# Gate rows by way of DRAM, the convolution's copies, taps and mean, and the low weight parts at the end of the recurrence, in a transformer block with convolution and HGRN2 layers

## The reference

```python
def forgetting_attention(q, k, v, f_logit):        # 8 heads of 64
    logf = jax.nn.log_sigmoid(f_logit)
    c = jnp.cumsum(logf, axis=1)                    # one running sum per head
    logits = q @ k.T * scale + c[query] - c[key]    # causal
    ...

def first_block(...):
    proj = rmsnorm(x) @ w_in                        # 3592 columns: q, k, v, 8 gates, q, k, v
    y = concat(forgetting_attention(...), chunked_relpos_attention(...))   # 8 + 8 heads
    x = x + rmsnorm(y @ w_out)
    x = x + rmsnorm(memory_cross_attention(...))    # 4 heads of 256, 256 memory rows
    x = x + rmsnorm(square(relu(rmsnorm(x) @ w_ff1)) @ w_ff2)              # 4096 wide

def conformer_conv(h, w_in, dw_w, dw_b, ln_g, ln_b, w_out):
    a, gate = jnp.split(h @ w_in, 2, axis=-1)
    u = a * jax.nn.sigmoid(gate)
    y = depthwise_conv(u, dw_w, width=31) + dw_b    # each channel by itself
    y = jax.nn.silu(layer_norm(y, ln_g, ln_b))
    return y @ w_out

def second_block(...):                              # mod = silu(c) @ ada_w + ada_b
    for i in range(2):
        h = modulate(rms_norm(x), sh1, sc1)
        y = conformer_conv(h) if i == 0 else hgrn2_mixer(h)
        x = x + g1 * y
        x = x + g2 * sq_relu_mlp(modulate(rms_norm(x), sh2, sc2))
    return rms_norm(x, final_g)
```

## Time and profile before

| | |
|---|---|
| median of 3 runs | 2173.49 us (2171.63, 2173.49, 2174.91) |
| profiled execution, its own time | 2178.39 us |
| its span in the profile | 2176.6 us, 26819 instructions |
| PE busy | 2111.1 us, 97% |
| DVE busy | 1244.8 us, 57% |
| ACT busy | 831.9 us, 38% |
| POOL busy | 199.3 us, 9% |
| one tap on VectorE (L2065), mean of 100 | 0.755 us |
| one centre on GpSimd (L2268), mean of 4 | 1.38 us |
| one addition to the mean on GpSimd (L2287), mean of 6 | 1.29 us |
| GpSimd's first eight bias sums, four each of heads 0 and 1, (L2236) end at | 80.85 us |

### The profile page before, as it was taken

One profiled execution on the slowest core, in us unless ns is written; L12 is line 12 of the kernel. 1 busy time (PEld: TensorE's weight loads), 2 busy tenths in 40 slices (PEclk: granted clock), 3 DMA queues, 4 the chain that ended last, 5 costly groups with the idle time before them and its releaser, 6 DMA issues.

```text
span 2176.6 us, 26819 instructions
## 1 busy us (share of the span) xinstructions
PE 2111.1 (97%) x10748; PEld 1657.1 (76%) x10748; DVE 1244.8 (57%) x1895; ACT 831.9 (38%) x1337; POOL 199.3 (9%) x170
## 2 busy tenths in 40 slices
PE   8999999999999999998999999999999989999998
PEld 7777887678878876665788888777777767888886
DVE  5555755446667777887554344376675755443443
ACT  5344544345323233224333233244454444232331
POOL 1221001011000004442100000100000000000001
PEclk9999999999999999999999999999999999999999
DMA  6113332024777762562232332221121222323321
GB/s 196 59 59 98 119 115 78 29 69 165 251 245 250 265 244 90 147 151 79 78 117 96 97 99 95 72 69 49 59 70 48 71 77 87 124 97 97 97 97 39
DMA packets 217691, 241.75 MB, mean 111 GB/s; under 512 B 10080, under 2 KB 204128, under 8 KB 211424
## 3 DMA queue, kind: packets, MB, share of 16 engines
q1 hardware_dynamic: 207248, 229.06, 32.3%
q10 hardware_dynamic: 10320, 10.97, 2.0%
HBM read 229.01 MB, written 2.10 MB: 106 GB/s over the span
## 4 chain that ended last, share of the span: by engine, by line
PE 84%; DVE 7%; ACT 4%; issue 2%; DMA 2%; ACTq 1%; POOL 0%; DVEq 0%; SPq 0%; POOLq 0%
PE bank L1225 23%; PE bank L1226 22%; PE bank L1227 22%; PE bank L1246 2%; PE bank L1247 2%; PE bank L1248 2%; PE bank L1425 1%; DVE wL L1813 1%; PE bank L1298 1%; PE bank L1353 1%; PE bank L1311 1%; PE bank L1291 1%; PE bank L1402 1%; DVE aacc L2008 1%; ACTq L1658 1%
## 5 line engine op out<-in xcount | busy, mean ns | idle before, releaser
L1225 PE MATMUL bank<-hH,wH 128*128 128x512 f32 (+1 forms) x1672 | 665.9, 398 | 25.3 <-DVE wL L1819 8.5
L1227 PE MATMUL bank<-hH,wL 128*128 128x512 f32 (+1 forms) x1672 | 648.2, 388 | 0.0
L1226 PE MATMUL bank<-hL,wH 128*128 128x512 f32 (+1 forms) x1672 | 647.9, 388 | 0.0
L1461 ACT ACTIVATE wH<-raw 128x1024 fp32r<-128x1024 f32 (+1 forms) x376 | 332.7, 937 | 360.4 <-PE bank L1227 269.5
L1813 DVE TENSOR_TENSOR wL<-raw,wH 128x1024 fp32r<-128x1024 f32 (+1 forms) x340 | 372.9, 1139 | 134.1 <-ACT wH L1461 134.1
L1225 PEld LDWEIGHTS bank<-hH,wH 128*128 128x128 f32 x1672 | 316.2, 189 | 117.6 <-issue 38.1
L1226 PEld LDWEIGHTS bank<-hL,wH 128*128 128x128 f32 x1672 | 316.7, 189 | 64.3 <-issue 3.8
L1227 PEld LDWEIGHTS bank<-hH,wL 128*128 128x128 f32 x1672 | 316.2, 189 | 64.7
L1225 PE MATMUL bank<-hidH,wH 128*128 128x512 f32 x768 | 299.8, 390 | 3.7 <-DVE hidL L1988 3.7
L1227 PE MATMUL bank<-hidH,wL 128*128 128x512 f32 x768 | 299.5, 390 | 0.0
L1226 PE MATMUL bank<-hidL,wH 128*128 128x512 f32 x768 | 299.4, 390 | 0.0
(11 more groups left out here) (219 smaller groups left out, 2075.0 us busy)
## 6 DMA issues: line engine op xcount, KB each, us to landing
raw<-in_mlp SPq DMA_DIRECT2D x64, 1024.0 KB, 5.3
araw<-in_ada_w SPq DMA_DIRECT2D x48, 1024.0 KB, 5.0
raw<-in_w_ff SPq DMA_DIRECT2D x32, 1024.0 KB, 7.4
raw<-in_hgrn_in SPq DMA_DIRECT2D x32, 512.0 KB, 3.8
raw<-in_w_in SPq DMA_DIRECT2D x11, 1024.0 KB, 5.4
raw<-in_conv_in SPq DMA_DIRECT2D x16, 512.0 KB, 5.2
u<-uc ACTq DMA_DIRECT2D x120, 67.5 KB, 3.2
raw<-in_w_mv SPq DMA_DIRECT2D x4, 1024.0 KB, 5.2
```

Of the source, the lines that this page charges most:

```text
L1225: mm(out, wH[:, s, m:m + 128], xh[:, k, 0:width], start=k == 0, stop=False)
L1226: mm(out, wH[:, s, m:m + 128], xl[:, k, 0:width], start=False, stop=False)
L1227: i = mm(out, wL[:, s, m:m + 128], xh[:, k, 0:width], start=False, stop=k == KB - 1)
L1461: do(wH[:, s, c], raw[:, r, c], ACT.Copy).then_inc(*s_whi.up(n, x))
```

## The change

**Gate rows.** The running sums are formed with their sign turned in `ev_gate`. SP writes the 8 rows to DRAM (`gate_rows`, 16 KB), and reads each head's row back, broadcast to 128 partitions (256 KB each). Heads 0, 1 and 4, 5 go to `cneg`, heads 2, 3 and 6, 7 to two blocks of `qk` that hold keys later (the keys' write waits for that head's last bias). `sel`, the 8 spreading matmuls and ScalarE's 8 copies are gone. A pair's reads are requested one pair ahead, and so are the relative-position tables.

**Low parts.** The two halves of a piece's low part are owed, and emitted, one by one. Where `keep` is set, one half comes after k = 2 and one at the next `take`; elsewhere all come after k = 2 as before. TensorE waits for a piece's parts inside the loop over k, ahead of its first use.

**Convolution.** Blocks 0 and 7: SP issues the copies of shifts 0 and 1, ScalarE those of 2 and 3. Blocks 1 to 6: ScalarE writes the padded u to DRAM (`conv_u`, one DMA), waits until it has landed, and reads the four shifted copies from there (four DMAs). All blocks have 15 taps on VectorE and 16 as matmuls. The mean is taken over blocks 0 to 5 and its matmul stands ahead of the last projection; GpSimd centres blocks 0 to 5 and squares 3 to 5, ScalarE squares the others; VectorE centres 6 and 7 straight from the bank; `ln_rest` sums blocks 6 and 7; the two additions are gone and there is a variance matmul for every block. The idle matmuls ahead of and behind the mean are gone; four stand behind the last variance matmul. The high parts of `conv_out`'s pieces come behind the last block's copies.

**End of the recurrence.** `hgrn_out` goes step by step (`step=1`); the splits of heads 0 to 2 stand ahead of level 7 and those of 3 to 5 behind it; head 6's norm and gate come after those; the last sum over a head comes two steps earlier in `hgrn_out`.

```diff
 def conv_first(blk):
-    return 15 if blk < KB - 1 else 11
+    return 15
...
     def highs(self, n):
         while self.made < n:
             self.do("weight_hi", n=self.made)
-            self.owed.append(self.made)
+            self.owed += [(self.made, 0), (self.made, 1)]
             self.made += 1
...
-    def lows(self):
-        for n in self.owed:
-            self.do("weight_lo", n=n)
-        self.owed.clear()
+    def lows(self, most=99):
+        for n, x in self.owed[:most]:
+            self.do("weight_lo", n=n, x=x)
+        del self.owed[:most]
...
-                    if k == 2 and not keep:
-                        self.lows()
+                    if k == 2:
+                        self.lows(1 if keep else 99)
...
+    def decays(self, p):
+        for h in (2 * p, 2 * p + 1):
+            self.chead[0, h] = 2 * (p % 2) + h % 2
+            self.do("decay", h=h, sc=self.chead[0, h], n=p // 2 + 1,
+                    cfree=(("pool", "bias", (0, h - 4, 3)),) if p > 1 else ())
...
         for blk in range(KB):
             slots[blk], free = shifts.get()
+            final = blk == KB - 1
             if blk:
-                run(self.linear(("a", blk), "conv_in", 0, 128 * blk, 128, src, to_a, nc_=128))
+                run(self.linear(("a", blk), "conv_in", 0, 128 * blk, 128, src, to_a, nc_=128, keep=final))
                 do("wdiag", blk=blk, k0=conv_first(blk), slot=slots[blk], after=free)
+                if final:
+                    mean()
+                    for j in range(3):
+                        do("ln_square", j=j)
+                    owed, self.owed = self.owed, []
...
+            if not direct(blk):
+                do("park", blk=blk)
+            if final:
+                do("shift_first", blk=blk, slot=slots[blk], after=free)
             do("shift", blk=blk, slot=slots[blk], after=free)
...
-        do("busy", tag="mean", n=3, b=b, after=after, x=True)
-        do("ln_mean", b=b, after=(), total=self.acc, s=s, free=free)
...
-        do("busy", tag="copies", n=2, b=b, after=after, x=True)
...
+        b, after = self.lin.get()
+        do("busy", tag="root", n=BUSY, b=b, after=after, x=True)
...
         last_h = len(self.pieces) - 1
         self.lows()
-        for j in range(KB - 1):
+        out = self.linear("hgrn_out", "hgrn_out", 0, 0, 1024, ("h", "ho"), self.to_x("r1x", (1, 2), "m1x", True), fresh=4,
+                          step=1)
+        for j in range(3):
             split(j)
-        out = self.linear("hgrn_out", "hgrn_out", 0, 0, 1024, ("h", "ho"), self.to_x("r1x", (1, 2), "m1x", True), fresh=4)
-        for _ in range(2):
-            next(last)
-            next(out)
+        next(last)
+        for j in range(3, KB - 2):
+            split(j)
+        final[0]()
+        end(ends[KB - 2])
+        split(KB - 2)
+        next(out)
+        next(out)
+        next(last)
...
         run(last)
+        sums(KB - 1)
         next(out)
-        sums(KB - 1)
...
-                elif kind == "decay":
-                    h = it["h"]
-                    pe.wait_ge(*s_dve.at("gate", 6))
-                    pe.wait_ge(s_sel, LANDED)
-                    mm(banks[it["b"]][:], view(sel, h, [[0, 128]]), tmp[0:8, plan.gate_slots[0], :], start=True,
-                       stop=True).then_inc(*s_mm.up("decay", h))
...
+                elif kind == "park":
+                    blk = it["blk"]
+                    act.wait_ge(*s_dve.at("u", blk))
+                    act.wait_ge(*s_pool.at("pad"))
+                    act.e.dma_start(a["u"][blk], uc[:, blk, :]).then_inc(s_ud[blk % 2], LANDED)
...
+                        act.wait_ge(s_ud[blk % 2], LANDED * (blk // 2 + blk % 2))
+                    for s in () if direct(blk) else range(4):
+                        act.e.dma_start(u4[32 * s:32 * s + 32, x, :, :],
+                                        bass.AP(tensor=a["u"].tensor, offset=128 * row * blk + s,
+                                                ap=[[row, 32], [32 * row, 4], [1, T + 28]])).then_inc(s_u4[x], LANDED)
...
-                    e.tensor_tensor(yc[:, j, :], yc[:, j, :], tmp[:, it["s"], :], SUB).then_inc(*s_dve.up("cen", j))
...
+                    e.scalar_tensor_tensor(out=yc[:, j, :], in0=banks[it["b"]][:], scalar=-1.0 / (128 * EARLY),
+                                           in1=yc[:, j, :], op0=MUL, op1=ADD).then_inc(*s_dve.up("cen", j))
...
+                elif kind == "rows":
+                    sp.wait_ge(*s_dve.at("gate", 6))
+                    dma(a["rows"], tmp[0:8, plan.gate_slots[0], :]).then_inc(s_rows, LANDED)
+                elif kind == "decay":
+                    sp.wait_ge(s_rows, LANDED)
+                    for ev in it["cfree"]:
+                        sp.wait_ge(*event(ev))
+                    h = it["h"]
+                    dma(gates(it["sc"]), bass.AP(tensor=a["rows"].tensor, offset=T * h, ap=[[0, 128], [1, T]])).then_inc(
+                        s_decay[it["sc"]], LANDED)
```

More of the change, by code:

```diff
@@ L235, in linear @@
             span = max(nc_, 128 * group)
-            ns = [self.take(name, k0, c0 + c + x, nc_, ahead=x == 0) for x in range(0, span, nc_)]
+            ns = [self.take(name, k0, c0 + c + x, nc_, ahead=ahead and x == 0, keep=keep) for x in range(0, span, nc_)]
             if self.beside is not None:
@@ L371, in pair @@
             self.do("bias", u=u)
-            if g == 0 and i == 3:
-                self.cslots.put(u["sc"], ("pool", "bias", u["id"]))
         yield
@@ L1176, in modgain, with copied, direct_copies @@
             return modA[:, 16 * lay + 8 * i + j:16 * lay + 8 * i + j + 1]
+        def copied(blk):
+            return LANDED * sum(16 if direct(i) else 4 for i in range(blk % 2, blk + 1, 2))
+        def direct_copies(queue, blk, x, shifts):
+            for s in shifts:
+                for g in range(4):
+                    queue.dma_start(u4[32 * s:32 * s + 32, x, g, :], uc[32 * g:32 * g + 32, blk, s:s + T + 28]).then_inc(
+                        s_u4[x], LANDED)
         def event(ev):
```

246 lines of the change are left out of this document (133 added, 113 removed).

## The result

The changed kernel took 2157.95 us by the median of four runs (2156.44 to 2162.07), the kernel before 2173.6 us by four; the ratio is 0.9932, with a 95% interval from 0.9915 to 0.9949. So it is faster, by 15.7 us by these medians (14.8 by the ratio) instead of the forecast 29.3. Timed again beside other kernels it came to 0.9923 (0.991 to 0.9935). The profiled execution of the changed kernel took 2156.95 us, with a span of 2155.2 us, 21.4 us shorter than the span before.

A forecast was written before the change was run, and what follows sets the result against it. TensorE, busy 97% of the span, was taken as the bound. Terms of 7.6 + 3.3 + 7.3 + 1.7 + 4.2 + 5.2 = 29.3 us off 2178.4 gave 2149.1, less 4.9 for the reference: 2144 us, range 2135 to 2158.

The forecast's parts named there:

- a wait for u4 in blocks 1 to 5: Convolution: TensorE waiting there for the shifted copies of u would show the forecast wrong; 4.8 us of spare time was claimed.
- Gate rows, -7.6 us: Attention: gate sums by way of DRAM take 8 matmuls off TensorE, four pairs of heads at 1.91 us each.
- rival (b): Attention: TensorE stops being the bound, softmax comes late and the 7.6 us turn into waits; 2152 us, 12%.
- rival (a): Clock falls follow something other than length of standing, so four shares of 1.7 us stay; 2151 us, 15%.
- Block 0, -3.3 us: Convolution's front: sharing copy issues removes 2.0 us of wait and 1.7 of clock; a later weight fetch costs 0.4.
- Blocks 1 to 6, 0 us: Convolution: copies through DRAM take 8.4 us within 13.2 us of cover, so nothing is gained or lost.
- Rival (d): Convolution's tap matmuls: the DRAM round trip outlasts its cover, costing six times the excess; 2161 to 2185 us, 3%.
- Tail, -7.3 us: Convolution's end: last projection's end to restart shrinks from 32.5 to 25.2 us, mean's matmul included.
- The tail's clock, -1.7 us: Restart after the convolution: four idle matmuls leave some 2 us standing, so lost clock is 1.7 us, not 3.4.
- Halved low parts, -4.2 us: Recurrence: 1.2 us off the first gather's wait, 1.7 of clock, 1.3 off the other six gathers; VectorE pays nothing.
- End of the recurrence, -5.2 us: Restart there: wait 2.1 instead of 3.9 us, 1.7 us less lost clock, and a later 1.67 us wait goes.
- The price of a wait in clock: TensorE: clock loss priced from neighbouring waits: 3.4 us after 5.71 us, 1.7 after 2.28, none after 1.92.

The follow-up runs named there:

- end_only: The kernel before with only the new order at the end of the recurrence: 2169.03 us, ratio 0.9976.
- halves_head0: The changed kernel with one weight fetch ahead of the sync queue's block 0 copies, and halved low parts only through the recurrence's first head: 2146.98 us, 0.9875.
- spread_kept: The changed kernel with eight matmuls on 8 rows, their result used by nobody, put back beside the DRAM way: 2167.53 us, 0.9967.

## Why the prediction was wrong

The forecast was 2144 us with a range from 2135 to 2158; the median of 2157.95 us is at the range's very end, and the gain was half of the forecast. It had named a wait for u4 in blocks 1 to 5 as a sign of being wrong, and that wait came. By the prediction's own steps:

- **Gate rows, -7.6 us: right, and somewhat small.** The matmuls' time came off in full, no new wait of TensorE appeared, and the reads were early enough; rival (b) did not come. (The other sign of being wrong, a wait between 40 and 200 us, was ill chosen: the wait near 195 us is there before too, at 204.58.) "Between 0 and 1.7 us for the clock I take 0" was the wrong end: alone the part gave 9.8 us (7.0 to 12.6), and no profile without the matmuls has a fall before 150 us. One stretch at full clock behind one pair of heads was weak evidence, since the falls come at another pair from profile to profile. The half of rival (a) that says that falls follow something else than standing holds here.
- **Block 0, -3.3 us: right** (3.9 us). The fetch behind the eight issues was seen, and wrongly priced: "0.4 us, bounds 0 and 2". I asked when TensorE wants the weights, and not what stands behind the late high part on ScalarE. The sigmoid of block 1 does, and it is the start of the next term.
- **Blocks 1 to 6, 0 us: wrong, 6.6 us.** This is the step that failed by most. The trip was priced at 8.4 us, with landings of 2.1 us (the output's) and 3.3 us (the median of the copies from SBUF), and with u in time. It took 9.5 to 12.1 us at blocks 2 to 6 and 15 us at block 1, chiefly because the last of four reads lands some 6 us after its issue even at the quiet blocks. So the spare time was 1 to 4 us and not 4.8. At block 1, u was 2.4 us late by the fetch, and the last read took 8.5 us beside fetches that had been pushed to the same moment. Rival (d) had the right place and mechanism, but at six blocks, where it happened at one. The Trainium skill (DMA: Bandwidth & Descriptors, Anatomy of one DMA) says, of DMAs that GpSimd issues, that the confirmation of a write to HBM can be surprisingly long. Here ScalarE issues them, and the trace agrees: from the write's issue to the reads' it took 4.4, 4.1, 2.4, 2.4, 2.4 and 4.9 us at blocks 1 to 6. At block 6 it was longest and TensorE did not wait, so the write was some part of the delay at block 1, not its cause.
- **Tail, -7.3 us: right.** 25.2 us from the projection's end against 24.3; with the mean and block 6's wait, which the term included, -6.5 us. The reason given was incomplete: without the way by DRAM the tail is some 5 us longer, by ScalarE's issues.
- **The tail's clock, -1.7 us: right in number by luck.** The row of 3.4 us counts 1.2 us that fell into the wait, where they cost nothing, so a single fall left over would have gained only some 0.5 us. The profiled execution of the changed kernel had no fall at the restart; of the nine profiled kernels with the idle matmuls at that place six have one, behind waits of 2.28 to 2.35 us, where its own was 2.35.
- **Halved low parts, -4.2 us: wrong.** The two terms of the first gather held (1.2 and 1.7 us); the fall behind it stands in four of the five profiles with whole low parts there (end_only has none) and in none of the nine with halves. The third, half of the other gathers' waits, came as 0.6 us (2.7 to 2.1) instead of 1.3, and "the halves are the same in number and size, so VectorE pays nothing" left out what a half moved to the next `take` does: TensorE waits 0.40 us for it four times, and the raw buffer comes free later, so that the next fetch goes out 3.4 us later. By itself the part gave no gain at all.
- **End of the recurrence, -5.2 us: right by itself** (5.2 us, first wait 1.92 us for 2.1), but only 3.3 us in the whole, by the fetch that the halves made late.
- **The point of reference: uncertain by some 2 us.** I took 4.9 us off, because the profiled execution was that far above the median of three. More runs put the kernel before at 2176.24, 2175.52 and 2173.96 us (21, 9 and 17 runs). The profiled execution was 2.1 to 4.4 us above these, so 0.5 to 2.8 us of the miss may come from a median of three.
- **The price of a wait in clock: chance.** It was read from neighbours of like length. In the same place the same wait brings a fall in some executions and none in others: 2.7 us at 608 to 622 us in six of fourteen profiles, 1.65 us at 411 to 425 us in five.
- One small slip: by the prediction's own numbers the round trip decides the sign from 15.1 us on (29.3 / 6 + 10.2), not 15.8.

Of the 14 us between forecast and result, 8 stand between the traces: 6.6 are block 1, about 5 the halves with what they do to the end, 0.8 the tail; the gates' surplus (1.8), block 0's (0.6) and the chance fall at 422 us (1.6) went the other way. The other 6 lie in which executions were profiled: the one before was 4.9 us above its median, the one after 1.0 us below. With the two fetches mended, halves_head0 reaches 2147 us, 3 us from the forecast.

## What to carry to other kernels

When an issue or a half-finished job is moved ahead of a prefetch, or holds its buffer longer, follow the late fetch past its first user: to the instruction that waits for it, to whatever stands behind that instruction on its engine, and to the next job that starts there. A hidden transfer's cover should be compared with its landing when other traffic is on the queues, not with the landing in a quiet place, and with the landing of the last of several copies, not with a median. And a median of three runs is no reference for a change of 1%, where single executions differ by 0.4%.

## What was not expected of the hardware

The granted clock fell while TensorE was busy without a gap: 0.51 over 67 to 71 us of spread_kept, at matmuls on 8 rows, at about 1.7 us a fall, in all five profiles that have such matmuls and in none of nine others between 60 and 150 us. The same copies from DRAM to SBUF landed within 5.9 us in one kernel and within 8.5 us in another, where only the place of one fetch differed (part of the convolution from 860 to 900 us).
